# Two token parts of 256 and 264, and one 512-column matmul for the weights' high part, in a split-precision decoder step

## The chip, the cores and the metric

The kernel runs on one core of one Trainium2 chip. Its metric is the device time of one launch in microseconds (us), the median of several runs. The core has five engines that run side by side and meet at semaphores: TensorE (PE, with its weight loads shown apart as PEld), VectorE (DVE), ScalarE (ACT), GpSimd (POOL) and SyncE (SP, which issues DMAs). TensorE writes its results to PSUM, eight banks of 512 fp32 columns for each of 128 partitions; DVE and ACT read them out ("evict" them) to SBUF.

## The reference: what is computed

Two layers of a decoder trunk for 512 prompt tokens and 8 sample tokens, all in fp32. Cut to what matters here:

```python
# layer 0: x (520 x 1024)
z = x @ w_in_e            # 3592 columns: gated short convolution, mLSTM q k v, gates
out = concat(conv_part, mlstm_part) @ w_out_e
# layer 1
z = x @ w_in_o            # 2236 columns: two sparse attentions and an indexer
out = concat(o_nsa, o_dsa) @ w_out_o
# both layers
x = layer_norm(ALPHA * x + out)
x = layer_norm(ALPHA * x + square(relu(x @ w_up)) @ w_down)   # w_up 1024 x 4096
```

The products with the six weight arrays make up nearly all of the time.

## The kernel before

**Split products.** Activations and weights are each split into a high part in fp32r and a low part (the remainder, again in fp32r). A product is made of three: high weights by high activations, high weights by low activations, low weights by high activations. `split_pass` (L1010 to L1029) does this: for each of eight blocks `k` of 128 input rows and each of the three, it issues one matmul for each token half. The activations lie transposed, features on partitions and the 520 tokens along the columns, so each matmul streams 260 columns (`H2 = T // 2`). A tile, numbered `g`, is 128 output features; it takes 8 x 3 x 2 = 48 matmuls and two PSUM banks (`bank(g, half)`), one for each half, in which the three products are summed. There are 191 tiles: 29 of the even input projection (from `G_IN0`), 8 of its output projection (`G_OUT0`), 64 of the first MLP (`G_MLP0`: four chunks of 8 "up" and 8 "down" tiles), 18 of the odd input projection (`G_IN1`), 8 of its output projection (`G_OUT1`) and 64 of the second MLP (`G_MLP1`).

**Weights.** SP loads weights into the three slots of `ring`. For each tile ACT writes the high part (`w_hi`, a copy of 128x1024, at L1599), and then DVE, for some tiles POOL, writes the low part (`w_lo`, L1972), which waits for ACT's copy. `w_hi_ahead` and `w_lo_ahead` do this some tiles ahead; they stand inside the step of the tile whose results are just being evicted, so they are in line behind that eviction on their engine. `weights_here` makes PE wait for both parts.

**Evictions.** In an up tile (`hidden`) ACT takes the first half out with a relu (L1636) and DVE the second (L1996); then POOL squares in fp32 (L842), ACT squares to the high part `hh` (L1643), and DVE subtracts to get the low part `hl` (L2001). In a down or output tile (`residual`) DVE adds both halves to `xT` (L1983, L1984). In the even projection ACT copies the first half and DVE the second (L2291).

**Heads and tails.** Around a layer norm the halves run apart, so that the norm of one half lies under products of the other. `tail` runs the last tiles of a stage for the first half, then for the second. `head` runs the first tiles of the next stage for the first half; the last pieces of the second half's norm (reciprocal L2042, multiplication L2051, affine step L2068, low part L2070 on DVE; centring L808 on POOL; affine steps L1670 on ACT) stand between the evictions of the head's tiles. At an MLP's head the step of tile j for j = 0 to 3 also prepares the weights of tile j + 4.

The order on each engine is that of the code; each engine works through it in line. The matmul that all of this goes through:

```python
last = pe.matmul(bank(g, half)[0:width(g), 0:H2], w[:, k, :], x[:, k, cols(half)],
                 start=first, stop=final)
```

Of the kernel before, what the change touches and what calls it, by code (L numbers as in the profile page):

```python
# [20 lines left out]
F32 = mybir.dt.float32  # L21
# [12 lines left out]
H2 = T // 2  # L34
# [43 lines left out]
def build(nc, x_prompt, x_sample, state_conv, state_C, state_n, state_m, cache_kv, cache_idx, cache_win, page_table,  # L78
# [20 lines left out]
    with ExitStack() as ctx:  # L99
# [11 lines left out]
        with ExitStack() as mixer:  # L111
            big = mixer.enter_context(nc.sbuf_tensor("big", [P, KF, T], F32))
            ymix = mixer.enter_context(nc.sbuf_tensor("ymix", [P, KD, T], F32))
            cbuf = mixer.enter_context(nc.sbuf_tensor("cbuf", [P, 4096], F32))
        with ExitStack() as odd:

            odd.enter_context(nc.sbuf_tensor("projections", [P, len(O_NAMES) * T], F32))
            xl1 = odd.enter_context(nc.sbuf_tensor("xl1", [P, KD, T], F32R))
            odd.enter_context(nc.sbuf_tensor("behind", [P, (KF - KD - len(O_NAMES)) * T], F32))
            xh1 = odd.enter_context(nc.sbuf_tensor("xh1", [P, KD, T], F32R))  # L120


        xh = sb("xh", [P, KD, T], F32R)
        xl = sb("xl", [P, KD, T], F32R)
        hh = sb("hh", [P, KD, T], F32R)
        hl = sb("hl", [P, KD, T], F32R)
# [12 lines left out]
        def piece(n):  # L139
# [13 lines left out]
            pn_ok dsd_ev pb_mm pb_ev pt_mm pt_ev kc_ok pc_mm vf_mm vf_ev pc_n pct_mm q_sc q_mm kv_out  # L153
# [248 lines left out]

        def cols(half):
            return slice(half * H2, (half + 1) * H2)

# [14 lines left out]
        def hid_event(c, j, half=None):  # L420

            return j + KD * half if c == 0 else KD * (c + 1) + j

# [87 lines left out]
        XL = {0: xl, 1: xl1, 2: xl}  # L511
        racc = att[:, 0:T]
# [220 lines left out]
        def _(pool):  # L733
# [98 lines left out]
            def hidden(layer, g, c, j, half=None):  # L832
# [3 lines left out]
                if half != 1:  # L836
                    pool.wait_ge(sm["free_a"], g + 1)
# [22 lines left out]
            for k in range(KD):  # L860
                if k not in XE_DVE:
                    pool.wait_ge(sm["tin_a"], k + 2)
                    pool.wait_ge(sm["tin_b"], 1)
                    pool.tensor_tensor(hl[:, k, :], xT[:, k, :], xh1[:, k, :].bitcast(F32), ALU.subtract).then_inc(sm["xe_p"], 1)
# [114 lines left out]
        def _(pe):  # L979
# [32 lines left out]
            def split_pass(gs, halves, hi, lo, ready_hi=None, ready_lo=None, between=None, ks=range(KD)):  # L1012

                for g in gs:
                    weights_here(g)
                for k in ks:
                    for part, ready, x in ((0, ready_hi, hi), (0, ready_lo, lo), (1, None, hi)):
                        if ready:
                            ready(k)
                        first, final = k == ks[0] and x is hi and part == 0, k == ks[-1] and part == 1  # L1020
# [1718 lines left out]
```

## Time and profile before

| | |
|---|---|
| median of 3 runs | 1429.27 us (1426.93 to 1429.67) |
| span of the profiled execution | 1421.2 us |
| PE busy | 1366.7 us, 96% |
| DVE busy | 745.3 us, 52% |
| ACT busy | 504.6 us, 36% |
| POOL busy | 397.1 us, 28% |
| mean granted TensorE clock | 0.994 |

The span runs from the first to the last instruction of one execution; the time of a run also holds what lies around it. PE's busy time counts overlapping matmuls, so its pace is read from the distance of their starts. A row of the timeline gives the start, the duration (of several merged instructions together), the engine, the line, the operation with output and inputs, and in brackets how long the engine was idle before and who ended it.

### The profile page before, as it was taken

What the parts mean: (1) busy time and instruction counts of PE and PEld (TensorE: products, weight loads), DVE (VectorE), ACT (ScalarE), POOL (GpSimd) and SP (SyncE); (2) the same over time, 40 slices, a digit from 0 to 9 for tenths busy, and PEclk for the clock granted to TensorE, in tenths of its full rate; (3) what the DMA queues carried; (4) which work ended last, traced back from release to release, by engine and by line L of the source; (5) the groups of instructions that cost most, each with busy time, mean ns of one, the idle gap of its engine ahead of it and who ended that gap; (6) DMA issues with size and microseconds to landing.
All of it is one profiled execution on the core that took longest, in us unless ns stands there. A gap on an engine that the chain in (4) does not pass through costs nothing. (4 is left out here: it accounts for less than half of the span.)

```text
span 1421.2 us, 27641 instructions
## 1 busy us (share of the span) xinstructions
PE 1366.7 (96%) x11359; PEld 1287.3 (91%) x11359; DVE 745.3 (52%) x1378; ACT 504.6 (36%) x1004; POOL 397.1 (28%) x470
## 2 busy tenths in 40 slices
PE   6999998999999999999899999999999999999996
PEld 5999975899999999999899966667999999999996
DVE  3424777667434343343879856454774343343435
ACT  3321224345314023032542366786553032140311
POOL 3014423365101010014744473023652010010102
PEclk9999999999999999999999999999999999999998
DMA  5343170030323131312323226204113313132301
GB/s 156 125 114 107 43 238 6 3 119 31 126 83 117 63 119 60 119 60 52 60 90 60 64 82 216 61 2 120 64 56 120 119 60 119 60 119 69 110 31 60
DMA packets 87196, 123.86 MB, mean 87 GB/s; under 512 B 24438, under 2 KB 42302, under 8 KB 87040
## 3 DMA queue, kind: packets, MB, share of 16 engines
q1 hardware_dynamic: 82048, 107.00, 23.6%
q0 software_dynamic: 5024, 15.10, 3.6%
q8 instruction: 91, 1.49, 0.4%
q14 instruction: 33, 0.27, 0.1%
HBM read 115.62 MB, written 8.57 MB: 87 GB/s over the span
## 5 line engine op out<-in xcount | busy, mean ns | idle before, releaser
L1024 PE MATMUL ps<-xh,ring_lo 128*128 128x260 f32 (+2 forms) x2496 | 503.5, 283 | 1.4 <-ACT big L1599 1.4
L1024 PEld LDWEIGHTS ps<-xh,ring_lo 128*128 128x128 f32 (+2 forms) x2496 | 382.6, 187 | 3.3 <-ACT big L1599 2.3
L1024 PE MATMUL ps<-xl,wr 128*128 128x260 f32 x1568 | 351.4, 283 | 6.1 <-DVE xl L2070 3.9
L1024 PE MATMUL ps<-xh,wr 128*128 128x260 f32 x1568 | 352.9, 284 | 2.5 <-POOL xl L824 1.2
L1024 PEld LDWEIGHTS ps<-xl,wr 128*128 128x128 f32 x1568 | 255.2, 188 | 8.2 <-DVE xl L2070 5.1
L1024 PEld LDWEIGHTS ps<-xh,wr 128*128 128x128 f32 x1568 | 256.0, 188 | 5.0 <-ACT att L1636 1.4
L842 POOL TENSOR_TENSOR att<-att 128x520 f32<-128x520 f32 (+1 forms) x80 | 77.3, 967 | 548.6 <-DVE att L1996 521.5
L1972 DVE TENSOR_TENSOR ring_lo<-ring,wr 128x1024 fp32r<-128x1024 f32 (+1 forms) x144 | 192.1, 1337 | 62.1 <-ACT wr L1599 62.0
L1024 PE MATMUL ps<-hh,wr 128*128 128x260 f32 x1024 | 222.1, 283 | 0.0
L1024 PE MATMUL ps<-hh,ring_lo 128*128 128x260 f32 x1024 | 221.8, 283 | 0.0
L1024 PE MATMUL ps<-hl,wr 128*128 128x260 f32 x1024 | 221.7, 283 | 0.0
L1599 ACT ACTIVATE wr<-ring 128x1024 fp32r<-128x1024 f32 (+1 forms) x162 | 167.4, 1049 | 130.1 <-PE ps L1024 120.4
L1024 PEld LDWEIGHTS ps<-hh,wr 128*128 128x128 f32 x1024 | 164.5, 188 | 0.2 <-issue 0.2
L1024 PEld LDWEIGHTS ps<-hh,ring_lo 128*128 128x128 f32 x1024 | 164.5, 188 | 0.0
L1024 PEld LDWEIGHTS ps<-hl,wr 128*128 128x128 f32 x1024 | 164.0, 188 | 0.0
L1636 ACT ACTIVATE att<-ps 128x260 f32<-128x260 f32 x64 | 24.6, 384 | 304.4 <-PE ps L1024 304.4
L1983 DVE TENSOR_TENSOR xT<-xT,ps 128x260 f32<-128x260 f32 x96 | 37.5, 422 | 162.9 <-PE ps L1024 162.9
L1996 DVE TENSOR_SCALAR att<-ps 128x260 f32<-128x260 f32 x64 | 27.4, 428 | 137.4 <-PE ps L1024 137.4
L1024 PE MATMUL ps<-hl,ring_lo 128*128 128x260 f32 (+1 forms) x464 | 93.4, 283 | 0.0
L1599 ACT ACTIVATE big<-ps 128x260 f32<-128x260 f32 (+6 forms) x104 | 40.3, 402 | 148.5 <-PE ps L1024 133.2
L789 POOL TENSOR_TENSOR ring_lo<-ring,wr 128x1024 fp32r<-128x1024 f32 x18 | 43.3, 2412 | 109.8 <-ACT wr L1599 109.8
L986 PE MATMUL ps<-big 128*64 128x128 f32 (+3 forms) x504 | 66.7, 348 | 4.8 <-DVE small L2694 3.3
(354 smaller groups left out, 1620.8 us busy)
## 6 DMA issues: line engine op xcount, KB each, us to landing
ring<-in_w_up SPq DMA_DIRECT2D x16, 2048.0 KB, 7.9
ring<-in_w_down SPq DMA_DIRECT2D x16, 2048.0 KB, 7.9
ring<-in_w_in_e SPq DMA_DIRECT2D x9, 1024.0 KB, 5.6
ring<-in_w_in_e SPq DMA_DIRECT2D x2, 2048.0 KB, 8.8
ring<-in_w_out_e SPq DMA_DIRECT2D x2, 2048.0 KB, 8.8
ring<-in_w_in_o SPq DMA_DIRECT2D x16, 256.0 KB, 5.0
ring<-in_cache_kv POOLq DMA_DIRECT2D x32, 128.0 KB, 2.4
ring<-in_w_out_o SPq DMA_DIRECT2D x8, 512.0 KB, 8.9
```

What stands on the lines that cost most here:

```text
L789: pool.tensor_tensor(w_l, w_raw(u), w_h.bitcast(F32), ALU.subtract).then_inc(sm["w_lo_p"], 1)
L842: pool.tensor_tensor(hid[j % 2][:, cc], rel[j % 2][:, cc], rel[j % 2][:, cc], ALU.mult).then_inc(sm["hid_sq"], 1)
L986: return pe.matmul(out, lhsT, rhs, start=start, stop=stop, skip_group_check=True)
L1024: last = pe.matmul(bank(g, half)[0:width(g), 0:H2], w[:, k, :], x[:, k, cols(half)], start=first, stop=final)
L1599: return act.activation(out, in_, ACT.Copy, scale=scale)
L1636: act.activation(rel[j % 2][:, 0:H2], psA(g)[:, 0:H2], ACT.Relu).then_inc(sm["free_a"], 1)
L1972: dve.tensor_tensor(w_l, w_raw(u), w_h.bitcast(F32), ALU.subtract).then_inc(sm["w_lo"], 1)
L1983: last = (dve.tensor_tensor(x, x, y, ALU.add) if scale is None else dve.scalar_tensor_tensor(x, x, scale, y, ALU.mult, ALU.add))
L1996: dve.tensor_scalar(rel[j % 2][:, H2:T], psB(g)[:, 0:H2], 0.0, None, ALU.max).then_inc(sm["free_b"], 1)
```

## The change

The token parts become 256 and 264 columns (`HALVES`, `HW`). The high and the low activation part of a stage move into one buffer (`x2`, `h2`, `xe2`, `x12`), so that one access pattern can take both. Where `apart(g, half)` is true, for the first half of 165 of the 191 tiles, the two matmuls of the weights' high part become one of 512 columns, which writes two column ranges of one whole bank: high by high activations in one, high by low in the other. The third product adds to one of the ranges. It isn't done for the first tile of the even projection and of each MLP, the gate tile, four tiles that are scaled, and the odd input projection. The two ranges are summed at the eviction by DVE: with a reduction over pairs (`summed`), or in `residual` with a second addition. So the halves change hands: DVE takes the first half out, ACT the second, and in an up tile ACT now applies the relu to the first half in SBUF, after DVE's sum (new semaphore `rel_ok`).

```diff
-H2 = T // 2
+HALVES = (slice(0, 256), slice(256, T))
+HW = (256, T - 256)
...
+        def apart(g, half):
+
+            if half or g in (G_IN0, G_IN0 + GATE, G_MLP0, G_MLP1) or G_IN1 <= g < G_OUT1:
+                return False
+            return g >= G_OUT0 or not 16 <= E_TILE[g - G_IN0] < 20
...
                         for g in gs:
-                            w = w_split(split_of[g])[part]
+                            w = w_split(split_of[g])[part][:, k, :]
                             for half in halves:
-                                last = pe.matmul(bank(g, half)[0:width(g), 0:H2], w[:, k, :], x[:, k, cols(half)],
-                                                 start=first, stop=final)
+                                m = HW[half]
+                                out = bank(g, half)[0:width(g), 0:m]
+                                if not apart(g, half):
+                                    last = pe.matmul(out, w, x[:, n, k, cols(half)], start=first, stop=final)
+                                elif part:
+                                    last = pe.matmul(bank(g, half)[0:width(g), m:2 * m], w, x[:, hi, k, cols(half)],
+                                                     start=False, stop=final)
+                                elif n == lo:
+                                    both = bank(g, half)[0:width(g), :].rearrange("p (n t) -> p n t", n=2)
+                                    last = pe.matmul(both if hi == 0 else both[:, ::-1], w, x[:, :, k, cols(half)],
+                                                     start=k == ks[0], stop=False)
...
 # ACT, hidden
-                if half != 1:
-                    tile_done(g, 0)
+                if half != 0:
+                    tile_done(g)
+                    act.wait_ge(sm["free_b"], g)
...
-                    act.activation(rel[j % 2][:, 0:H2], psA(g)[:, 0:H2], ACT.Relu).then_inc(sm["free_a"], 1)
+                    act.activation(rel[j % 2][:, cols(1)], psB(g)[:, 0:HW[1]], ACT.Relu).then_inc(sm["free_b"], 1)
+                if half != 1:
+                    act.wait_ge(sm["free_a"], g + 1)
+                    act.activation(rel[j % 2][:, cols(0)], rel[j % 2][:, cols(0)], ACT.Relu).then_inc(sm["rel_ok"], 1)
                 if g + 1 != TAIL_OF[1]:
                     w_hi_ahead(g, 1 if half is None else half)
...
 # DVE
                 last = (dve.tensor_tensor(x, x, y, ALU.add) if scale is None
                         else dve.scalar_tensor_tensor(x, x, scale, y, ALU.mult, ALU.add))
+                if apart(g0 + m, half):
+                    link(last)
+                    last = dve.tensor_tensor(x, x, bank(g0 + m, half)[:, HW[half]:2 * HW[half]], ALU.add)
...
+            def summed(out, g, n=P):
+
+                if apart(g, 0):
+                    return dve.tensor_reduce(out, psA(g)[0:n, :].rearrange("p (n t) -> p t n", n=2), AX.X, ALU.add)
+                return dve.tensor_copy(out, psA(g)[0:n, 0:HW[0]])
...
 # DVE, hidden
-                    dve.tensor_scalar(rel[j % 2][:, H2:T], psB(g)[:, 0:H2], 0.0, None, ALU.max).then_inc(sm["free_b"], 1)
+                    summed(rel[j % 2][:, cols(0)], g).then_inc(sm["free_a"], 1)
                 if g + 1 != TAIL_OF[1]:
                     w_lo_ahead(g, 1 if half is None else half)
```

What stands in line on DVE at the head of an MLP, from the second half's variance to the second tile's step, before (L1972 is `w_lo`, L2001 `hl`, L2042 the reciprocal, L2051 the norm's multiplication):

```order
L2037 TENSOR_TENSOR att<-ps,att 128x260
L2038 TENSOR_SCALAR att<-att 128x260
L1972 TENSOR_TENSOR ring_lo<-ring,wr 128x8x128
L2001 TENSOR_TENSOR hl<-att,hh 128x260
L2042 RECIPROCAL att<-att 128x260
L2051 TENSOR_TENSOR xT<-xT,att 128x260 x2
L1972 TENSOR_TENSOR ring_lo<-ring,wr 128x8x128
L2001 TENSOR_TENSOR hl<-att,hh 128x260
```

The same place after the change (L2002 is `w_lo`, L2040 `hl`, L2081 the reciprocal, L2090 the multiplication, L2023 the new sum):

```order
L2040 TENSOR_TENSOR h<-att,h 128x256
L2081 RECIPROCAL att<-att 128x264
L2090 TENSOR_TENSOR xT<-xT,att 128x264 x2
L2023 TENSOR_REDUCE att<-ps 128x256
L2002 TENSOR_TENSOR ring_lo<-ring,wr 128x8x128
L2040 TENSOR_TENSOR h<-att,h 128x256
L2090 TENSOR_TENSOR xT<-xT,att 128x264 x2
```

The step of each head tile now begins with an eviction on DVE, ahead of `w_lo`.

ACT at the same place before (L1636 relu from PSUM, L1599 with `wr` the high weights `w_hi`, L1643 `hh`):

```order
L1636 ACTIVATE att<-ps 128x260
L1599 ACTIVATE wr<-ring 128x1024
L1643 ACTIVATE hh<-att 128x260
L1681 ACTIVATE att<-att 128x260
L1636 ACTIVATE att<-ps 128x260
L1599 ACTIVATE wr<-ring 128x1024
L1643 ACTIVATE hh<-att 128x260
```

and after (L1666 is the relu in SBUF, L1625 `w_hi`):

```order
L1707 ACTIVATE att<-ps 128x264
L1666 ACTIVATE att<-att 128x256
L1625 ACTIVATE wr<-ring 128x1024
L1673 ACTIVATE h<-att 128x256
L1711 ACTIVATE att<-att 128x264
```

The relu reads what DVE has summed, and the weights' high part stands in line behind it.

PE before, the last block of the first up chunk's last tile (second half alone) and one block `k` of a down tile with both halves:

```order
L1024 MATMUL ps<-xl,wr 128x260
L1024 MATMUL ps<-xh,ring_lo 128x260
L1024 MATMUL ps<-hh,wr 128x260 x2
L1024 MATMUL ps<-hl,wr 128x260 x2
L1024 MATMUL ps<-hh,ring_lo 128x260 x2
```

and after, one block of the down tile:

```order
L1044 MATMUL ps<-h,wr 128x264
L1050 MATMUL ps<-h,wr 128x512
L1044 MATMUL ps<-h,wr 128x264
L1046 MATMUL ps<-h,ring_lo 128x256
L1044 MATMUL ps<-h,ring_lo 128x264
```

Six matmuls of 1560 columns in all become five of 1560 columns.

## Rows read from the trace of the kernel before

**Rows 1.** The page: busy time of PE, and its granted clock in 40 slices.
```profile
PE 1366.7 (96%) x11359; PEld 1287.3 (91%) x11359; DVE 745.3 (52%) x1378; ACT 504.6 (36%) x1004; POOL 397.1 (28%) x470
...
PEclk9999999999999999999999999999999999999998
```
**Rows 2.** Busy times by stretch: PE, PEld, DVE, ACT, POOL, clock, DMA share, GB/s.
```profile
400.00:500.00 100.00, 100.00 (x834) 100.00 (x833) 37.27 (x51) 21.86 (x31) 8.43 (x8) 1.00 0.24 85
```
**Rows 3.** Timeline of DVE in the up tiles of an MLP chunk.
```profile
414.77 0.43 DVE L1996 TENSOR_SCALAR att<-ps 128x260 f32<-128x260 f32 x1 [3.99 <-PE ps L1024]
416.02 1.45 DVE L1972 TENSOR_TENSOR ring_lo<-ring,wr 128x1024 fp32r<-128x1024 f32 x1 [0.82 <-ACT wr L1599]
...
455.14 0.43 DVE L1996 TENSOR_SCALAR att<-ps 128x260 f32<-128x260 f32 x1 [2.46 <-PE ps L1024]
...
457.76 0.69 DVE L2001 TENSOR_TENSOR hl<-att,hh 128x520 fp32r<-128x520 f32 x1
```
**Rows 4.** Timeline of PE in the mLSTM: plain fp32 matmuls of several widths.
```profile
235.66 1.02 PE L986 MATMUL ps<-att 128*128 128x512 f32 x2
236.52 0.59 PE L986 MATMUL ps<-big 128*128 128x256 f32 x2
236.96 0.81 PE L986 MATMUL ps<-att,ones 128*128 128x384 f32 x2
237.60 0.81 PE L986 MATMUL ps<-att 128*128 128x384 f32 x2
```
**Rows 5.** Timeline of PE: from the gate tile (8 weight columns) to full tiles.
```profile
30.24 0.63 PE L1024 MATMUL ps<-xh,ring_lo 128*8 128x260 f32 x4
...
31.42 0.40 PE L1024 MATMUL ps<-hl,ring_lo 128*128 128x260 f32 x2
...
35.04 0.40 PE L1024 MATMUL ps<-hl,ring_lo 128*128 128x260 f32 x2
```
**Rows 6.** Groups of DVE instructions: a reduction of 512 elements.
```profile
L2429 DVE TENSOR_REDUCE small<-att 128x8 f32<-128x512 f32 x2 | 1.4, 686 | 0.1
```
**Rows 7.** Timeline of DVE at the head of the second MLP.
```profile
1037.75 0.43 DVE L2037 TENSOR_TENSOR att<-ps,att 128x260 f32<-128x260 f32 x1 [5.32 <-ACT att L1677]
...
1038.98 1.61 DVE L1972 TENSOR_TENSOR ring_lo<-ring,wr 128x1024 fp32r<-128x1024 f32 x1
...
1044.48 1.77 DVE L1972 TENSOR_TENSOR ring_lo<-ring,wr 128x1024 fp32r<-128x1024 f32 x1
...
1049.51 1.22 DVE L1972 TENSOR_TENSOR ring_lo<-ring,wr 128x1024 fp32r<-128x1024 f32 x1
...
1053.43 1.22 DVE L1972 TENSOR_TENSOR ring_lo<-ring,wr 128x1024 fp32r<-128x1024 f32 x1
```
**Rows 8.** Timeline of ACT at the same place.
```profile
1037.61 0.39 ACT L1636 ACTIVATE att<-ps 128x260 f32<-128x260 f32 x1
1037.87 1.07 ACT L1599 ACTIVATE wr<-ring 128x1024 fp32r<-128x1024 f32 x1
1038.82 0.43 ACT L1643 ACTIVATE hh<-att 128x260 fp32r<-128x260 f32 x1
```
**Rows 9.** PE's waits: waiter, who ended it, total us, times, longest.
```profile
PE ps L1024 <- DVE ring_lo L1972: 1.0, 2, 0.5
```
**Rows 10.** Timeline of DVE in the even projection's last tiles.
```profile
175.55 0.42 DVE L2291 COPY big<-ps 128x260 f32<-128x260 f32 x1
...
205.09 0.19 DVE L2312 TENSOR_TENSOR small<-small 128x32 f32<-128x32 f32 x1
```
**Rows 11.** Timeline of DVE in the first half of the even output tail.
```profile
279.38 1.25 DVE L1972 TENSOR_TENSOR ring_lo<-ring,wr 128x1024 fp32r<-128x1024 f32 x1 [1.44 <-ACT wr L1599]
280.56 0.75 DVE L1984 SCALAR_TENSOR_TENSOR xT<-xT,ps 128x260 f32<-128x260 f32 x2
```
**Rows 12.** Busy times by stretch, columns as in rows 2.
```profile
826.00:828.00 2.00, 0.53 (x4) 0.29 (x2) 1.82 (x7) 0.70 (x3) 0.59 (x2) 1.00 0.07 8
828.00:835.00 7.00, 6.58 (x35) 4.90 (x35) 1.96 (x8) 3.20 (x10) 7.00 (x11) 0.52 0.01 1
```

More of the change, by code:

```diff
@@ L114, in build @@
             cbuf = mixer.enter_context(nc.sbuf_tensor("cbuf", [P, 4096], F32))
+        with ExitStack() as even:
+            even.enter_context(nc.sbuf_tensor("projected", [P, (KF - KD) * T], F32))
+            xe2 = even.enter_context(nc.sbuf_tensor("xe2", [P, 2, KD, T], F32R))
         with ExitStack() as odd:
             odd.enter_context(nc.sbuf_tensor("projections", [P, len(O_NAMES) * T], F32))
[L118 to L126, printed above, removed]
+            x12 = odd.enter_context(nc.sbuf_tensor("x12", [P, 2, KF - len(O_NAMES), T], F32R))
+        x2 = sb("x2", [P, 2, KD, T], F32R)
+        h2 = sb("h2", [P, 2, KD, T], F32R)
+        xel, xeh = xe2[:, 0], xe2[:, 1]
+        xl1, xh1 = x12[:, 0], x12[:, 1]
+        xh, xl = x2[:, 0], x2[:, 1]
+        hh, hl = h2[:, 0], h2[:, 1]
         sb("gap", [P, KD * T + 4096 - NWS * KD * P])
@@ L1010, in weights_here, with split_pass @@
                 pe.wait_ge(sm[by], n)
-            def split_pass(gs, halves, hi, lo, ready_hi=None, ready_lo=None, between=None, ks=range(KD)):
+            def split_pass(gs, halves, x, order=(0, 1), ready_hi=None, ready_lo=None, between=None, ks=range(KD)):
+                hi, lo = order
                 for g in gs:
@@ L1029, in split_pass, with split_tile @@
                         between()
-            def split_tile(g, hi, lo, ready=None, between=None):
+            def split_tile(g, x, order=(0, 1), ready=None, between=None):
                 banks_free(g)
-                split_pass((g,), (0, 1), hi, lo, ready, between=between)
+                split_pass((g,), (0, 1), x, order, ready, between=between)
             def x_hi_here(n_ln, half):
@@ L1067, in head @@
                 first = n // 2
-                split_pass(range(g, g + first), (1,), XH[n_ln], XL[n_ln], x_hi_here(n_ln, 1), x_lo_here(n_ln, 1))
+                split_pass(range(g, g + first), (1,), *X[n_ln], x_hi_here(n_ln, 1), x_lo_here(n_ln, 1))
                 for i in range(first, n):
@@ L1203, in _ @@
                     for half in range(2):
-                        last = mm(ps[4 + half][0:4, 0:H2], ident[0:8, 4:8], gz[:, half * H2:(half + 1) * H2])
+                        last = mm(ps[4 + half][0:4, 0:HW[half]], ident[0:8, 4:8], gz[:, cols(half)])
                     last.then_inc(sm["fg_mm"], 1)
@@ L1313, in _ @@
                 if idx >= 4:
-                    split_tile(G_IN1 + idx, xh1, xl1, between=selected if idx == 4 else None)
+                    split_tile(G_IN1 + idx, x12, (1, 0), between=selected if idx == 4 else None)
                 if idx == 4:
@@ L1675, in moments @@
                 act.wait_ge(sm["stats_mm"], 2 * n_ln + half + 1)
-                copy(mu[:, cols(half)], ps[4 * half][:, 0:H2]).then_inc(sm["mu_ok"], 1)
-                act.activation(var[:, cols(half)], ps[4 * half][:, 0:H2], ACT.Square).then_inc(sm["sq_mu"], 1)
+                copy(mu[:, cols(half)], ps[4 * half][:, 0:HW[half]]).then_inc(sm["mu_ok"], 1)
+                act.activation(var[:, cols(half)], ps[4 * half][:, 0:HW[half]], ACT.Square).then_inc(sm["sq_mu"], 1)
             def deviation(n_ln, half):
@@ L1726, in _ @@
             act.wait_ge(sm["tin_b"], 1)
-            copy(xh1[:, :, S:T], xT[:, :, S:T]).then_inc(sm["tin_a"], 1)
+            copy(xeh[:, :, S:T], xT[:, :, S:T]).then_inc(sm["tin_a"], 1)
             for k in range(KD):
@@ L1750, in _ @@
                     act.wait_ge(sm["small_in"], 16 * 2)
[L1751 removed]
+                    act.activation(gz[:, cols(1)], psB(g)[0:8, 0:HW[1]], ACT.Identity, bias=gbc[0:8, :]).then_inc(sm["free_b"], 1)
                 else:
[L1753 removed]
+                    copy(big[:, home, cols(1)], psB(g)[:, 0:HW[1]], MH_SCALE if 16 <= t < 20 else 1.0).then_inc(sm["free_b"], 1)
                 w_hi_ahead(g)
@@ L1990, in hidden @@
                 cc = slice(0, T) if half is None else cols(half)
-                if half != 0:
-                    tile_done(g)
+                if half != 1:
+                    tile_done(g, 0)
                     if e >= 2:
```

81 lines of the change are left out of this document (41 added, 40 removed).

## The prediction

> **What bounds the kernel now.** First the page: PE is busy for 96% of the span at full granted clock [rows 1], so the question is what sets PE's pace and where it stands still. In a stretch of the first MLP PE issues 834 matmuls in 100 us with no gap, while DVE is busy for 37 us and ACT for 22 [rows 2]: there only PE counts. A finer pace comes from DVE's evictions of up tiles, which follow PE. From the first to the last of eight there are 40.37 us, seven tiles of 48 matmuls, so 5.767 us a tile and **120.15 ns a matmul** of 260 columns, 720.9 ns for the six of a block k [rows 3]. Second, where PE isn't alone: the heads of the two MLPs, where DVE works almost without a pause from 1037.75 on, with weight preparation, low parts and the second half's norm in one line [rows 7], and PE already waits for `w_lo` there, once in each head, 0.5 us each [rows 9]; and the last tiles of the even projection, where DVE runs as closely from 175.55 to 205.09 [rows 10]. At these places the change adds work to DVE.
>
> **What PE gains.** 165 tiles have 8 blocks each, so 1320 matmuls go, but no column goes: 1560 a block before and after. All hangs on how the 120.15 ns divide into a part for each instruction and a part for each column; the trace has one width of fp32r alone. Plain fp32 matmuls give a scale: start to start 0.43 us for 512 columns, 0.32 for 384, 0.22 for 256 [rows 4], so time by the column, 0.84 ns each, and next to nothing fixed. If fp32r streams at half of that, 260 columns are 109 ns (108.3 at one column in each cycle of the 2.4 GHz level), and 11.8 ns a matmul are left. If those are fixed, a block goes from 720.9 to 650 + 5 x 11.8 = 709 ns and **saves 11.9 ns**. If they belong to the columns it saves 0. Weight loads have a small share: with 8 weight columns ten matmuls take 1.18 us, 118 ns each, and thirty at 128 weight columns 3.62 us, 120.7 ns [rows 5]; with one load fewer this alone gives 2.7 ns. In the other direction the one long matmul may hide its neighbours' cost too: if the 512 columns ran with the 2 ns of the plain kind, the block would save 240.3 x 512/520 - 215.5 = 21 ns, and if its neighbour gained as well about 30. I take 11.9, between the ends 0 and 30, since the plain rows are the nearest and half their slope is what one column a cycle needs. The Trainium skill ("TensorE: Matmul & The Clock Gate", section "Back-to-back issue gap") gives N/2.4 plus about 2.5 ns for a stream of matmuls. The plain rows agree with so small a fixed part [rows 4]; fp32r at 120 ns doesn't follow it. By that rule the block would save 2.5 ns only. It speaks against the change and is the second case below.
>
> The gain counts where PE sets the pace. In the MLPs these are 126 tiles less the 14 merged ones in the heads: 112 x 8 = 896 blocks, **-10.7 us**. Both halves' evictions fit there: a tile takes 5.7 us, and DVE's work of 2.6 us in an up tile grows by 0.3.
>
> **The eviction in a steady up tile.** DVE's sum reads 512 elements; the nearest row is a reduction of 512 at 0.69 us [rows 6] against 0.43 for the copy it replaces. Then ACT's relu and, behind it, `w_hi`, then DVE's `w_lo` and `hl`. From the last eviction to the end of `hl` there are 3.31 us now [rows 3]. New: 0.69 + 0.03 + 0.28 (relu, start to next start) + 1.05 + 0.06 + 1.37 + 0.69 = 4.2 us. The down tile that follows reads this last part at its eighth block, after 7 x 0.709 = 5.0 us. Covered, with 0.8 us left; a sum of over 1.5 us would show eight times.
>
> **The heads: what DVE and ACT lose.** Before, ACT ran ahead with relu and `w_hi` (1037.61 and 1037.87 [rows 8]), and DVE came to a `w_lo` that could start at once. Now each head step on DVE is: sum, then wait until ACT has done the relu and `w_hi`, then `w_lo`. Nothing hides this bubble, since DVE works in line and ACT waits for DVE's sum. Bubble: 0.03 + 0.27 (1037.61 to 1037.87) + 1.05 + 0.06 = 1.41 us. The first tile isn't merged: copy 0.42 + 1.41 = 1.83 us. Tiles 1 to 3: 0.69 + 1.41 = 2.10 us each. The `w_lo` of step 3, which PE needs for tile 7, ended at 1053.43 + 1.22 = 1054.65 [rows 7]; PE was waiting for it. It comes 1.83 + 3 x 2.10 = 8.1 us later. PE is held at tile 5 (the `w_lo` of step 1 comes 3.9 us late), at tile 6 and at tile 7, its own gain of 0.1 us a tile is lost in the waits but for tile 7, and the second half starts 8.0 us late. From there PE isn't held again: the last low parts of the norm come about as much later as the second half starts later, and PE reads them at the end of a pass over four tiles of 4 x 24 x 122 ns = 11.7 us. Behind DVE's waits are also queued the norm's multiplications, but PE reads them later. Both MLP heads have the same row of steps: 2 x 8.0 = **+16.0 us**. Bounds: if the sum took 0.43 us (the present eviction) 2 x 7.2, if it took 1.2 (as long as the reductions' 512 elements twice over, less one overhead) 2 x 9.5.
>
> **The even projection.** 23 merged tiles. PE gains 17 x 8 x 11.9 ns = 1.6 us up to tile 22; then DVE's line sets the time. Six evictions from 175.55 to 205.09 [rows 10] grow by 0.27 us each, 1.6 us, and the two before take some of PE's lead. I count **+0.9 us**; bounds -1.5 (DVE's growth hidden) and +4 (a sum of 1.2 us).
>
> **The output tails.** In their first half a DVE step is now residual, wait for ACT's square and `w_hi`, `w_lo`: 3.0 us a step, of which the wait is 1.44 [rows 11]. The second addition adds 0.45 us, so the `w_lo` of step 3 ends 1.8 us later, at 282.4; PE reaches that tile at 282.45. PE keeps 6 x 8 x 11.9 = 0.57 us in each of two tails: **-1.1 us**. The last tile's residual is later by 0.45 and earlier by 0.6, and the norm's chain under the second half stays as it is. The second half isn't merged; its 264 columns against 260 are in the block's sum.
>
> **The sum.** -10.7 + 16.0 + 0.9 - 1.1 = +5.1 us on the span of 1421.2, so 1426.3. The median lies 8.1 above the span, 1429.27; on it the forecast is **1434.4 us**. (A measurement can tell about 0.2%, 2.9 us.)
>
> **The rivals.**
> - *The cost goes by columns.* Saving 0 to 5 ns a block: PE gains 0 to 4.5 us in the MLPs where I took 10.7, and 0 to 0.5 in place of 1.1 in the tails: 1441 at 5 ns, 1446 at 0. For it: the plain rows scale by columns. Against: half their slope doesn't reach 120 ns.
> - *The long matmul pays more than its own instruction (faster).* The mechanism is in PE's stream: while 512 columns run, the next weights are there early and the neighbours' 11.8 ns shrink. The heads cost 16.0 all the same. The sum is zero at 896s = 15.8 us, s = 17.6 ns a block; it is faster by over 0.2% from s = 21. At 21 it is 1426, at 30 some 12 us less than now less the tails, 1417. For it: the load starts with the matmul before it and lasts about as long as 260 columns; against: with 8 weight columns the pace is only 2.7 ns better.
> - *The heads' line isn't as I read it.* If DVE reached its sums while ACT's copies were already made, only the sums would count: 2 x (0.42 + 3 x 0.69) = 5.0 in place of 16, 1423. Against: the order after the change puts `w_hi` behind the relu, and the relu behind the sum.
> - *The clock falls in the heads.* After a stretch in which PE was busy 0.53 of 2.0 us the granted clock went to 0.52 for 7 us [rows 12], to the 1.2 GHz level. In the heads PE now stands for three times 3 to 4 us. A fall while it runs tile 7 and the group pass costs half of the time, 3.4 us a head: 1438 to 1441.
>
> **How the numbers follow.** The forecast as it stands, 1432.2 to 1438 with the bounds of the reduction's length: 0.35. Costs by column 0.14, the clock 0.09; with the forecast, all above 1432.2, that makes **slower 0.58**. Savings of 14 to 21 ns a block, or heads somewhat better than I read them, end within 0.2%: **same 0.22**. The long matmul's case beyond 21 ns 0.12 and the heads' case 0.08: **faster 0.20**. The range: above I leave out the purest column case (under 0.1), below the last of the faster cases (under 0.1): **1422 to 1445**.
>
> **What would show it.** PE: the distance of up-tile evictions in the steady MLP, 5.767 us now, should be 5.67; 5.73 or more means columns, 5.60 or less the faster case. The 512-column matmul, start to start: 225 ns, or 230 and more. DVE: a TENSOR_REDUCE of about 0.69 us, and in each MLP head four gaps of 1.4 us ended by ACT's `wr`. PE: three waits for DVE's `ring_lo` in each head, some 10 us together, where one of 0.5 us stood. The even projection's DVE line ends within a microsecond of 205. The clock row at 1.0 in the heads. I am wrong if the head gaps are hidden, if the reduction takes over 1 us, or if the pace moves by more than 0.17 us a tile or not at all.

## The result

The changed kernel takes **1439.3 us** (median of 4 runs, 1438.03 to 1442.34), the kernel before 1428.8 in the runs beside it (4 runs, 1426.93 to 1429.67): a ratio of 1.0086, 95% interval 1.0064 to 1.0108, so 10.5 us are added where the forecast had 5.1. The time is inside the range and on the side forecast. The profiled spans are 1421.2 and 1436.4 us, 15.2 apart.

The page of the changed kernel, busy times and granted clock in 40 slices, against [rows 1]:

```profile
PE 1370.4 (95%) x10039; PEld 1229.3 (86%) x10039; DVE 788.0 (55%) x1458; ACT 531.1 (37%) x1068; POOL 394.8 (27%) x470
...
PEclk9999999999999999999999999999999999999998
```

1320 matmuls have gone and PE is busy no shorter. The steady part of the first MLP, against [rows 2] (PE, PEld, DVE, ACT, POOL, clock, DMA share, GB/s) and, in the timeline of DVE, against [rows 3]:

```profile
400.00:500.00 100.00, 100.00 (x702) 93.84 (x701) 42.25 (x63) 24.06 (x38) 8.44 (x8) 1.00 0.27 97
```
```profile
424.64 0.69 DVE L2023 TENSOR_REDUCE att<-ps 128x256 f32<-128x512 f32 x1 [3.37 <-PE ps L1046]
426.76 1.23 DVE L2002 TENSOR_TENSOR ring_lo<-ring,wr 128x1024 fp32r<-128x1024 f32 x1 [1.43 <-ACT wr L1625]
427.91 0.69 DVE L2040 TENSOR_TENSOR h<-att,h 128x520 fp32r<-128x520 f32 x1
...
464.63 0.69 DVE L2023 TENSOR_REDUCE att<-ps 128x256 f32<-128x512 f32 x1 [1.75 <-PE ps L1046]
```

Seven tiles from 424.64 to 464.63 are 39.99 us: 5.713 us a tile, where it was 5.767. A block costs 714.1 ns instead of 720.9, and **6.8 ns are saved** where the forecast had 11.9. From start to start on PE, over the up and down tiles between 410 and 650 us, the 512-column matmuls take 232.2 ns on average (225 forecast), those of 264 columns 121.9 and those of 256 columns 116.8; in the kernel before 260 columns take 120.2. The sum takes the 0.69 us forecast, and `hl` ends 3.96 us after the sum starts (4.2 forecast), under PE's work.

DVE's timeline in the head of the second MLP, against [rows 7]:

```profile
1048.74 0.43 DVE L2076 TENSOR_TENSOR att<-ps,att 128x264 f32<-128x264 f32 x1 [5.37 <-ACT att L1707]
1049.21 0.30 DVE L2077 TENSOR_SCALAR att<-att 128x264 f32<-128x264 f32 x1
1049.42 0.42 DVE L2024 COPY att<-ps 128x256 f32<-128x256 f32 x1
1051.27 1.56 DVE L2002 TENSOR_TENSOR ring_lo<-ring,wr 128x1024 fp32r<-128x1024 f32 x1 [1.43 <-ACT wr L1625]
...
1055.48 0.78 DVE L2090 TENSOR_TENSOR xT<-xT,att 128x264 f32<-128x264 f32 x2
1056.17 0.68 DVE L2023 TENSOR_REDUCE att<-ps 128x256 f32<-128x512 f32 x1
1058.29 1.50 DVE L2002 TENSOR_TENSOR ring_lo<-ring,wr 128x1024 fp32r<-128x1024 f32 x1 [1.44 <-ACT wr L1625]
...
1065.31 1.23 DVE L2002 TENSOR_TENSOR ring_lo<-ring,wr 128x1024 fp32r<-128x1024 f32 x1 [1.43 <-ACT wr L1625]
...
1070.39 1.50 DVE L2002 TENSOR_TENSOR ring_lo<-ring,wr 128x1024 fp32r<-128x1024 f32 x1 [1.43 <-ACT wr L1625]
```

The four waits for ACT's `wr` are there, 1.43 or 1.44 us each. PE's waits for `w_lo` (waiter, who ended it, total us, times, longest), and PE's timeline at the three of the first head (0.72, 3.71 and 2.30 us; the second head has two, 0.72 and 3.71, and the sixth, 0.42, stands at 1011 us in the odd output tail):

```profile
PE ps L1050 <- DVE ring_lo L2002: 11.6, 6, 3.7
```
```profile
333.14 0.47 PE L1050 MATMUL ps<-x,wr 128*128 128x512 f32 x1 [0.72 <-DVE ring_lo L2002]
...
339.89 0.47 PE L1050 MATMUL ps<-x,wr 128*128 128x512 f32 x1 [3.71 <-DVE ring_lo L2002]
...
345.23 0.77 PE L1050 MATMUL ps<-x,wr 128*128 128x512 f32 x1 [2.30 <-DVE ring_lo L2002]
345.79 0.41 PE L1046 MATMUL ps<-x,ring_lo 128*128 128x256 f32 x1
346.00 0.63 PE L1050 MATMUL ps<-x,wr 128*128 128x512 f32 x1
```

After the third wait the 512-column matmuls start 0.64 us after one another together with their neighbour, where before the wait it was 0.35: the granted clock has fallen to the 1.2 GHz level. Three stretches at that level, columns as in rows 2 with the length of the stretch first (two more, 3.4 us at 204.9 and the last 9.5 us of the span, lie where PE has little to do):

```profile
344.80:348.20 3.40, 2.97 (x9) 2.62 (x10) 2.67 (x7) 1.45 (x4) 0.17 (x1) 0.51 0.02 5
1065.00:1071.80 6.80, 5.12 (x16) 4.30 (x16) 5.02 (x8) 5.07 (x10) 1.35 (x3) 0.50 0.00 0
822.70:836.40 13.70, 13.70 (x72) 11.22 (x71) 4.52 (x15) 4.83 (x16) 5.41 (x10) 0.50 0.08 14
```

**Where the 15.2 us of span are.** The marks are starts on DVE: its first subtraction of the mLSTM's scores, the first step of each half's variance (L2037 before, L2076 after), and the first and last of its custom instructions in the attention stage.

| stage | before | after | difference | of which |
|---|---|---|---|---|
| start to the scores (even projection) | 206.6 | 208.3 | +1.7 | 0.7 lies ahead of PE's wait near 50 us, 1.0 behind it |
| to the variance, half 0 (mLSTM, output tail) | 83.7 | 84.6 | +0.9 | the tail |
| to half 1 | 29.0 | 29.0 | 0 | |
| to the next norm (first MLP) | 359.4 | 364.2 | +4.8 | 448 blocks -3.05; head +7.8 |
| odd projection, two marks | 133.9 | 133.7 | -0.2 | |
| attention | 159.9 | 162.4 | +2.5 | clock low for 13.7 us, before for 6.8 [rows 12] |
| to the variance (odd output tail) | 36.2 | 37.5 | +1.3 | the tail |
| to half 1 | 29.0 | 29.0 | 0 | |
| second MLP to the end | 383.5 | 387.7 | +4.2 | 448 blocks -3.05; head and the rest +7.3 |

The changed kernel's profiled run took 1438.03 us, 1.6 above its span and 1.3 below its median. The span of before lies 7.6 us below the median beside it, so if the same 1.6 us lie around it, its profiled run was some 6 us faster than the median. That is why medians differ by less than spans. Most of the spread among runs of one kernel goes with the mean granted clock: of 23 runs of the kernel before that stood beside the last timed experiments, those at 0.987 took 1431.4 to 1432.6 us, those at 0.991 1426.9 to 1429.6, those at 0.995 1422.1 and 1423.4. Single microseconds are therefore read from stages in the traces, not from medians.

### The profile page after: what moved, and what is told of

It reads as the page before. It is cut to its first block and busy times, and to the rows that moved or that the text cites. A ratio compares the mean times of both kernels' runs of the same rounds, so it can differ in the third digit from the quotient of the medians.

```text
span 1436.4 us, 25209 instructions
## 1 busy us (share of the span) xinstructions
PE 1370.4 (95%) x10039; PEld 1229.3 (86%) x10039; DVE 788.0 (55%) x1458; ACT 531.1 (37%) x1068; POOL 394.8 (27%) x470
## 5 line engine op out<-in xcount | busy, mean ns | idle before, releaser
L1044 PE MATMUL ps<-x,wr 128*128 128x264 f32 (+3 forms) x1888 | 410.0, 285 | 5.7 <-DVE x L2109 3.7
L1044 PEld LDWEIGHTS ps<-x,wr 128*128 128x128 f32 (+1 forms) x1888 | 306.0, 187 | 9.2 <-DVE x L2109 4.9
L1044 PE MATMUL ps<-h,wr 128*128 128x264 f32 x1024 | 271.9, 284 | 0.0
L1050 PE MATMUL ps<-x,wr 128*128 128x512 f32 x624 | 239.7, 401 | 12.9 <-DVE ring_lo L2002 11.6
L1044 PE MATMUL ps<-x,ring_lo 128*128 128x264 f32 (+3 forms) x944 | 240.6, 284 | 0.0
L2002 DVE TENSOR_TENSOR ring_lo<-ring,wr 128x1024 fp32r<-128x1024 f32 (+1 forms) x144 | 181.3, 1263 | 106.3 <-ACT wr L1625 106.1
L1625 ACT ACTIVATE wr<-ring 128x1024 fp32r<-128x1024 f32 (+1 forms) x162 | 167.0, 1046 | 112.1 <-PE ps L1044 97.8
L1050 PE MATMUL ps<-h,wr 128*128 128x512 f32 x512 | 197.8, 394 | 0.6 <-DVE h L2040 0.6
L1044 PEld LDWEIGHTS ps<-h,wr 128*128 128x128 f32 x1024 | 186.3, 188 | 0.1
L1046 PE MATMUL ps<-x,ring_lo 128*128 128x256 f32 x624 | 173.2, 282 | 0.0
L1044 PEld LDWEIGHTS ps<-x,ring_lo 128*128 128x128 f32 (+1 forms) x944 | 165.7, 187 | 0.0
L1044 PE MATMUL ps<-xe,ring_lo 128*128 128x264 f32 (+2 forms) x840 | 158.0, 287 | 1.9 <-DVE big L2023 1.9
L1046 PEld LDWEIGHTS ps<-x,ring_lo 128*128 128x128 f32 x624 | 119.1, 191 | 18.4
L1050 PEld LDWEIGHTS ps<-h,wr 128*128 128x128 f32 x512 | 96.3, 188 | 5.1 <-issue 0.9
```

What stands on the lines that cost most here:

```text
L1044: last = pe.matmul(out, w, x[:, n, k, cols(half)], start=first, stop=final)
L1046: last = pe.matmul(bank(g, half)[0:width(g), m:2 * m], w, x[:, hi, k, cols(half)], start=False, stop=final)
L1050: last = pe.matmul(both if hi == 0 else both[:, ::-1], w, x[:, :, k, cols(half)], start=k == ks[0], stop=False)
L1625: return act.activation(out, in_, ACT.Copy, scale=scale)
L2002: dve.tensor_tensor(w_l, w_raw(u), w_h.bitcast(F32), ALU.subtract).then_inc(sm["w_lo"], 1)
```

## The experiments

**The parts alone.** The changed kernel with the halves of 256 and 264 and with its new order of evictions, but no matmul merged:

```diff
 def apart(g, half):
-    if half or g in (G_IN0, G_IN0 + GATE, G_MLP0, G_MLP1) or G_IN1 <= g < G_OUT1:
-        return False
-    return g >= G_OUT0 or not 16 <= E_TILE[g - G_IN0] < 20
+    return False
```

> The changed kernel without any 512-column matmul: parts of 256 and 264 tokens, six matmuls a block, the evictions in their new hands (DVE takes the first half out with a copy or one addition, ACT the second, and in an up tile ACT applies the relu to the first half in SBUF behind DVE's copy). Theory (the heads' line on DVE and ACT costs the time, the long matmul gives some back): a tile of an MLP at the old 5.77 us, no gain on PE, and in each MLP head four steps of 0.42 + 1.43 us, 7.4 us a head; in all some 1443 us, 14 over the kernel before. Rival (it is the sums of two ranges, the extra DVE reading, that cost): without them the time is that of the kernel before, 1429.

1441.8 us (6 runs), ratio 1.0097 (1.0066 to 1.0128). By the medians the merging itself gains 2.5 us over this kernel. By the stages it gains 0.7 and 3.3 us in the two MLPs, and loses 1.0 in the even projection and 1.2 and 1.6 in the two output tails, so next to nothing in the sum. What loses against the kernel before is the new order: the two MLP stages take 364.9 and 391.0 us, where they took 359.4 and 383.5. The steady pace, 5.77 us a tile, is that of before. DVE, up tiles:

```profile
420.32 0.42 DVE L2022 COPY att<-ps 128x256 f32<-128x256 f32 x1 [3.87 <-PE ps L1042]
422.17 1.23 DVE L2000 TENSOR_TENSOR ring_lo<-ring,wr 128x1024 fp32r<-128x1024 f32 x1 [1.43 <-ACT wr L1623]
...
426.08 0.42 DVE L2022 COPY att<-ps 128x256 f32<-128x256 f32 x1 [2.07 <-PE ps L1042]
```

**Merging off in the heads only**, the order as in the changed kernel:

```diff
-    if half or g in (G_IN0, G_IN0 + GATE, G_MLP0, G_MLP1) or G_IN1 <= g < G_OUT1:
+    if half or g in (G_IN0, G_IN0 + GATE) or G_IN1 <= g < G_OUT1:
+        return False
+    if G_MLP0 <= g < G_MLP0 + KD or G_MLP1 <= g < G_MLP1 + KD:
         return False
```

> The changed kernel with the 512-column matmul off in the first half of the eight head tiles of each MLP; the line of DVE, ACT and the weights there is as in the changed kernel. Theory (the bubble of DVE waiting for ACT's relu and high weights is the larger part, the longer sum the smaller): each of three head steps gets 0.27 us shorter, 0.8 us a head, some 1437.7 us. Rival (the sum itself is what the heads lose): most of the 11 us come back, 1430.

1436.5 us (12 runs), ratio 1.0050 (1.0030 to 1.0069). Nearer to the theory, though the two MLP stages are only 0.6 and 0.3 us shorter, where 0.8 each were expected. PE still waits 9.5 and 0.4 us for `ring_lo`: with plain copies most of the loss stays, since the four waits of 1.43 us a head stay.

**ACT makes `w_hi` ahead of the relu**, merging as in the changed kernel:

```diff
+                if half == 0:
+                    w_hi_ahead(g, 0)
                 if half != 1:
                     act.wait_ge(sm["free_a"], g + 1)
...
-                if g + 1 != TAIL_OF[1]:
+                if half != 0 and g + 1 != TAIL_OF[1]:
                     w_hi_ahead(g, 1 if half is None else half)
```

> The changed kernel with one move: in the first half of an MLP head ACT makes the next high weights (w_hi) before it waits for DVE's sum and applies the relu, not behind it. Everything else, the sums and the 512-column matmuls too, stays. Theory (the bubble is the price): four bubbles of 1.43 us a head go, 5.7 us a head, 11.4 in all, so some 1428 us; no gap of 1.43 us ended by ACT's wr is left on DVE in the heads. Rival (DVE's own work bounds the heads): under 3 us come back, 1437.

1426.3 us (12 runs), ratio 0.9995 (0.9970 to 1.0020). By the medians the move gives 13 us back. The two MLP stages take 358.2 and 383.0 us, where the changed kernel has 364.2 and 387.7: **10.7 us** less, 11.4 expected, of which 1.4 is the low clock of the first head. Another 2.6 us lie in the attention stage, where the clock was low for 6.8 us and not for 13.7; they aren't the move's. The kernel is level with the one before. DVE in its first head: `w_lo` follows the copy at once, and in each step only a wait of 0.5 us for POOL's square is left. PE still waits for `w_lo` twice in each head, 2.3 us together, where the kernel before has 0.5.

```profile
322.46 0.42 DVE L2026 COPY att<-ps 128x256 f32<-128x256 f32 x1
322.79 1.21 DVE L2004 TENSOR_TENSOR ring_lo<-ring,wr 128x1024 fp32r<-128x1024 f32 x1
324.51 0.97 DVE L2042 TENSOR_TENSOR h<-att,h 128x256 fp32r<-128x256 f32 x1 [0.50 <-POOL att L858]
```

**Columns or instructions.** At the end of the changed kernel PE also runs seven trains of 32 fp32r matmuls, each matmul with weights of its own and the other engines nearly idle (so the kernel does more than the reference asks):

```diff
+for s, k in probe:
+    pe.matmul(ps[6][:, 0:256], wr[:, s, k, :], flow[:, 520 * k:520 * k + 256], ...)
```

> The changed kernel with seven trains of 32 fp32r matmuls each, added at the end behind PE's last transposes, when the other engines are nearly idle: 260, 512, 512 in two ranges, 384 and 256 columns with 128 weight columns, then 260 and 512 columns with 8 weight columns, new weights each time. Fixed-cost theory: about 12 ns over N/2.4 at every width, 225 ns at 512 and 118 at 256. Column theory: 0.45 ns a column at every width, 232 at 512, 174 at 384, 116 at 256. If other engines' traffic or the weight loads made the difference, the trains run at N/2.4 + 2 ns: 215 at 512, and with 8 weight columns faster than with 128.

PE's timeline, a row for each train (32 matmuls; starts 231.9 ns apart where a train of 512 columns takes 7.42 us to the next one's start):

```profile
1424.46 4.08 PE L1617 MATMUL ps<-ring_lo,wr 128*128 128x260 f32 x32
1428.39 7.59 PE L1619 MATMUL ps<-ring_lo,wr 128*128 128x512 f32 x32
1435.81 7.59 PE L1621 MATMUL ps<-ring_lo,wr 128*128 128x512 f32 x32
1443.25 5.73 PE L1623 MATMUL ps<-ring_lo,wr 128*128 128x384 f32 x32
1448.82 3.95 PE L1625 MATMUL ps<-ring_lo,wr 128*128 128x256 f32 x32
1452.61 3.98 PE L1627 MATMUL ps<-ring_lo,wr 128*8 128x260 f32 x32
1456.42 7.57 PE L1629 MATMUL ps<-ring_lo,wr 128*8 128x512 f32 x32
```

Start to start: 512 columns 231.9 ns, read as one range or as two (L1619, L1621); 384 columns 5.57 us / 32 = 174.1; 256 columns 3.79 / 32 = 118.4; and with 8 weight columns 260 take 3.81 / 32 = 119.1, with 128 of them 119.9 (after the train's first matmul, which overlaps the transposes). That is 0.453, 0.453 and 0.463 ns a column for 512, 384 and 256: **nearly all of the cost goes by columns**. The 512 and 384 columns match the column theory (232 and 174), the 256 alone the fixed-cost theory's 118. Two of 256 are 236.8 ns, one of 512 231.9, so merging saves 4.9 ns in a train, and not the 11.8 of the forecast. Whether one range is read or two makes no difference, and 8 weight columns instead of 128 make 0.8 ns at 260 columns.

**The heads as before the change** (ACT evicts the first half, no merging in the heads), the rest as changed:

```diff
+                if half == 0:
+                    tile_done(g, 0)
+                    act.activation(rel[j % 2][:, cols(0)], psA(g)[:, 0:HW[0]], ACT.Relu).then_inc(sm["free_a"], 1)
...
-                if half != 1:
+                if half is None:
...
                     summed(rel[j % 2][:, cols(0)], g).then_inc(sm["free_a"], 1)
```

> The changed kernel, but the heads of the two MLPs work as in the kernel before: their tiles are not merged, and ACT makes the relu of the first half out of PSUM, ahead of w_hi, while DVE evicts nothing there. The rest is merged as in the changed kernel. Theory: e3_whi_first (1426.25 us) still has DVE's copy and three sums in the line of each head, 2.5 us of waits on w_lo where the kernel before has 0.5; taking them out gives 2 x 2.0 us back, and the heads' own merging gain of 2 x 7 x 8 x 6.8 ns = 0.8 us is lost: 1423. What is left against before is the gain of the steady MLP (6.1 us) less what the even projection and the output tails lose (1.7 + 2.2). Rival: what was left of the heads' loss in e3 is hidden by the norm under them, so that nothing more comes back: 1426 to 1427, as e3. The ratio to before is 0.996 by the theory and 0.9985 by the rival.

1428.0 us (12 runs), ratio 0.9996 (0.9980 to 1.0012): the median sides with the rival. The stages side with the theory: the two MLP stages take 356.7 and 381.5 us, against 358.2 and 383.0 with `w_hi` first, 3.0 us less (3.2 expected), and against 359.4 and 383.5 before. In the profiled run the difference is eaten elsewhere, by a clock that was low for 3.4 us at 212, 253, 700 and 840 us and for 13.7 at 820. By its median this kernel equals the one before; the heads' cost is shown by the stages. Against the changed kernel they are 7.5 and 6.2 us shorter.

**The output tails unmerged too**:

```diff
+    if G_OUT0 <= g < G_OUT0 + KD or G_OUT1 <= g < G_OUT1 + KD:
+        return False
```

> e5_heads_as_before, and the first half of the two output tails isn't merged either. Theory: after the second addition DVE hands the last x tiles over so late that the sums of the norm (POOL's chain) hold PE when it has done the first tile of the second half; without merging this wait of 1.1 us goes, and each tail ends 1.2 to 1.6 us earlier (0.90 + 0.27 and 1.26 + 0.35, the stage differences of the changed kernel and of e1_split_only against before): 2.8 us less than e5, about 1420. Rival, the line of the prediction: the norm's chain is not delayed and merging gains 0.4 us in each tail, so that the time rises by 0.7 us, to about 1424. Shown by the wait of norm_sums on att, 1.1 us in the first tail, and by the two stages' length.

**1422.5 us** (6 runs), ratio 0.9958 (0.9941 to 0.9974): faster than both kernels. The odd tail's stage goes from 37.5 to 35.9 us. PE's wait for the norm's sums, here and, second, in the kernel with tails merged:

```profile
PE ps L1008 <- POOL att L821: 0.4, 2, 0.2
```
```profile
PE ps L1006 <- POOL att L819: 2.1, 4, 0.9
```

The odd tail's 1.6 us are what was expected of it. In the even tail's stage both profiled runs have stretches of low clock, so that its part can't be read. 5.5 us between the medians are more than the 2.8 expected, and the mean clock doesn't explain it: the runs at 0.990 take 1426.5 to 1428.9 us there and 1421.8 to 1423.2 here. What makes up the rest stays open. Against the kernel before the gain is safer: the runs at 0.991 take 1420.9 and 1422.2 us here, and 1426.9 to 1429.6 there.

**Merging in the steady MLPs alone** (the even projection unmerged as well):

```diff
-    return g >= G_OUT0 or not 16 <= E_TILE[g - G_IN0] < 20
+    return G_MLP0 <= g < G_MLP0 + 2 * KF or g >= G_MLP1
```

> e6_tails_off, and the even projection isn't merged either: matmuls are merged only in the MLPs outside their heads. Theory: DVE's copies of 0.43 in place of sums of 0.69 in the last tiles of the even projection bring its end from 208.3 back to the 206.8 of e1_split_only, 1.5 us less than e6: about 1418.5, ratio to before 0.992, faster than both kernels. The step at the first score, 206.6 in the kernel before, tells it. Rival: PE's gain of 17 tiles x 8 x 6.8 ns = 0.9 us in the first tiles is lost with it and the stage's end is set by something else, so that the time stays at e6's within 0.5 us.

1423.0 us (12 runs, 1416.7 to 1427.8), ratio 0.9965 (0.9944 to 0.9986): again faster than both, but no different from the one before, where 1.5 us less were expected. From the start of PE's wait near 50 us to the scores it takes 156.8 us, against 157.8 in the kernels that merge there and 156.8 before: the even projection's merging costs 1.0 us, and this run began that stretch 1.7 us later than the other (50.9 against 49.3). That start lies anywhere from 49.3 to 51.4 us in the profiled kernels, with merging there and without.

**What DVE's instructions cost beside POOL.** In the heads the `w_lo` of step 3 came 6.2 us late, not 8.1, though each step grew as forecast. Two kernels, each with POOL's centring in the heads cut to 8 columns (this part of the computation is left out), the first from the kernel before, the second from the changed one:

```diff
-                        centre(n_ln, 1, range(4 * j, 4 * j + 4))
+                        for m in range(4 * j, 4 * j + 4):
+                            pool.wait_ge(sm["mu_ok"], 2 * n_ln + 2)
+                            pool.tensor_tensor(xT[:, m, T - 8:T], xT[:, m, T - 8:T], mu[:, T - 8:T],
+                                               ALU.subtract).then_inc(sm["cen_p"], 1)
```

> The kernel before, but in the heads of the two MLPs POOL subtracts the mean in the last 8 columns of the second half instead of all 260 (eight instructions a head; this part of the computation is left out). Theory: while POOL's four subtractions of 4.1 to 4.4 us run, DVE's instructions beside them take up to twice their time (w_lo 1.61 and 1.77 us against 1.22 without, hl 0.97 against 0.42, the pair on xT 1.36 and 1.73 against 0.77). Without them the w_lo of step 3 ends about 3.6 us earlier after the second half's variance than now: 13.3 us instead of 16.9, and PE's wait for ring_lo in the heads goes (0.3 us left at most). Rival: those DVE instructions take their time by themselves (the first touch of new tiles), whatever POOL does: 16.9 us stays. The time itself moves by 1 us or less either way.

> The changed kernel with the same cut: POOL subtracts the mean in the last 8 columns of the second half only, in the heads of the MLPs. In the changed kernel the w_lo of step 3 ends 23.15 us after the variance, 6.2 later than in the kernel before, where the four steps grow by 1.85 + 3 x 2.11 = 8.2. Theory: the missing 2 us are DVE's time beside POOL that the waits of 1.43 us have taken over; with the cut DVE's instructions are short in both kernels, so this one saves only some 2.9 us (23.15 to 20.2) against 3.6 of the kernel before, and the difference between the two comes nearer to 8.2 (7 or more). Rival: POOL has no part in it, the end stays at 23.15 and the difference at 6.2. The sum of the four waits for ACT's wr stays at 4 x 1.43 by both.

DVE's timeline in the second head, from the variance to the `w_lo` of step 3; the kernel before with the cut, then the changed one with it:

```profile
1039.33 0.43 DVE L2040 TENSOR_TENSOR att<-ps,att 128x260 f32<-128x260 f32 x1 [5.33 <-ACT att L1680]
...
1040.56 1.23 DVE L1975 TENSOR_TENSOR ring_lo<-ring,wr 128x1024 fp32r<-128x1024 f32 x1
1041.71 0.42 DVE L2004 TENSOR_TENSOR hl<-att,hh 128x260 fp32r<-128x260 f32 x1
...
1043.85 0.77 DVE L2054 TENSOR_TENSOR xT<-xT,att 128x260 f32<-128x260 f32 x2
...
1051.47 1.21 DVE L1975 TENSOR_TENSOR ring_lo<-ring,wr 128x1024 fp32r<-128x1024 f32 x1
```
```profile
1046.51 0.43 DVE L2079 TENSOR_TENSOR att<-ps,att 128x264 f32<-128x264 f32 x1 [5.38 <-ACT att L1710]
...
1065.39 1.50 DVE L2005 TENSOR_TENSOR ring_lo<-ring,wr 128x1024 fp32r<-128x1024 f32 x1 [1.43 <-ACT wr L1628]
```

From the variance to the end of that `w_lo` there are 13.35 us (13.3 expected; 16.9 uncut) and 20.38 (20.2 expected; 23.15 uncut). The difference rises from 6.25 to 7.0. A `w_lo` of 1.61 us becomes 1.23 and `hl` 0.42 instead of 0.97: **these DVE instructions take longer beside POOL's**. The rival falls. Of the 1.2 us that are still missing to 8.2, most lie where POOL's squares and low parts run beside DVE in the first kernel and not in the second (two affine steps of 0.71 and 0.72 us against 0.40 and 0.42, a low part of 0.85 against 0.43). No wait of PE for `ring_lo` is left in the heads of the first kernel, as expected; its two MLP stages are 0.8 us shorter each than before. The Trainium skill ("SBUF — State Buffer", section "Who interferes with whom") has the same rule: a DVE instruction with two SBUF inputs contends with a GpSimd instruction that reads SBUF, and one blocks the other. These rows agree for `w_lo`, `hl` and the multiplications on `xT`. The times were 1423.6 and 1434.6 us, with 1428.1 for the kernel before beside them, in a single run each, which tells nothing of single microseconds.

The first of these kernels, which has nothing of the change, also ran 13.7 us at the low clock in the attention stage:

```profile
814.50:828.20 13.70, 13.70 (x72) 11.22 (x71) 4.46 (x15) 4.64 (x16) 5.27 (x10) 0.50 0.07 14
```

Its attention stage takes 162.4 us as well, and with `w_hi` first, where the clock was low for 6.8 us, it takes 159.8. So that row of the table above, 2.5 us, isn't the change's. The heads differ: in the five profiled kernels whose heads hold PE for 1.9 to 3.7 us at a time (the changed one, the first two experiments, the one with the trains, the last), the clock falls once in each head; in the six without such holds, in none.

## Why the prediction was right, and where it was not

**What PE gains (mis-sized).** 896 blocks by 6.8 ns are 6.1 us, not 10.7. The failed step is the split of 120.15 ns into 108.3 by column and 11.8 fixed. The slope of plain fp32 [rows 4] was halved, and that doesn't hold: fp32r has a slope of its own, about 0.45 ns, and little that is fixed. The rival of the columns had 0 to 5 ns a block; trains give 4.9, the kernel 6.8, nearer to it than to the forecast. Why the kernel saves 1.9 ns more than the trains is not shown. For the faster rival the forecast had a weight load last about as long as 260 columns; its rows last 0.19 us, against 0.12 from one matmul to the next. By the rule of the Trainium skill ("TensorE: Matmul & The Clock Gate", section "Back-to-back issue gap"), N/2.4 plus about 2.5 ns, 512 columns would take 215.8 ns and the block save 2.5. The prediction took it for a stream; that section gives it for a matmul by itself, and about 131 ns at 512 columns for a stream of weight loads and matmuls. The measured 231.9 and 118.4 ns follow neither; the small fixed part is nearer to the truth than mine.

**The steady eviction (right).** Sum 0.69, wait 1.43, `hl` done in 3.96 us. One thing was missed: in the last chunk of the second MLP the first two down tiles start as a pair of the tail, and PE reaches the low part earlier. It waits 0.6 us for `hl` there.

**The heads (right in mechanism, somewhat less).** The bubble was 1.43 us (1.41 forecast), the steps grow by 1.85 and 3 x 2.11 (1.83 and 2.10). The end of the fourth `w_lo` came 6.25 us late and not 8.1: behind the waits POOL's centring runs by itself, and DVE's later instructions are shorter (0.78 us for a pair on `xT` where it was 1.36, 1.50 for the second `w_lo` where it was 1.77 [rows 7]). The forecast moved the old durations unchanged. PE's waits are 6.7 us in the first head and 4.4 in the second, not 10. In the sum: 7.8 and about 6.7, together 14.5 where 16.0 stood, of which 1.4 is the clock. The kernel with its heads as before gives nearly the same by another way: its stages are 7.5 and 6.2 us shorter than the changed kernel's. The 1.36 is this row of the kernel before:

```profile
1043.20 1.36 DVE L2051 TENSOR_TENSOR xT<-xT,att 128x260 f32<-128x260 f32 x2
```

**The clock (a rival that came on top).** It fell in both heads, as that rival had it, but at less cost than its 3.4 us a head. In the first the low stretch starts 0.4 us before the third wait ends. The five pairs of matmuls behind the wait take 3.20 us, where the same five behind the second wait take 1.82: it costs 1.4. In the second it lies over tile 6, and PE's slow tile only fills what would have been the third wait: none is left there, since the `w_lo` sets the end either way. The kernel with the trains, the same as the changed one up to its end, bears this out: its first head has a low stretch of 6.8 us over tile 6, no third wait, and a first MLP stage of 362.8 us, 1.4 less than the 364.2 above.

**The even projection (right).** +1.0 us behind PE's wait near 50, +0.9 forecast. PE's last wait there, for DVE's copy before and for its sum after (total us, times, longest), and DVE's line after:

```profile
PE ps L986 <- DVE big L2291: 0.7, 1, 0.7
```
```profile
PE ps L1002 <- DVE big L2023: 2.1, 1, 2.1
```

```profile
201.54 0.69 DVE L2023 TENSOR_REDUCE big<-ps 128x256 f32<-128x512 f32 x1
...
206.84 0.19 DVE L2351 TENSOR_TENSOR small<-small 128x32 f32<-128x32 f32 x1
```

DVE's line ends at 206.84 against 205.09 [rows 10], not within a microsecond, for 0.7 of it was there already when PE's wait near 50 us began.

**The output tails (wrong, sign and all).** Forecast -1.1, measured +0.9 and +1.3. The step that failed is "the norm's chain under the second half stays as it is". PE's gain didn't reach the end, because the last tiles' residuals were no longer in PE's time but in DVE's. Before, POOL's last addition ended at 287.85, 0.65 us before PE came for it:

```profile
287.10 0.75 POOL L801 TENSOR_TENSOR att<-att 128x260 f32<-128x260 f32 x1
```

DVE, then POOL, then PE, in the changed kernel:

```profile
284.04 0.41 DVE L2014 SCALAR_TENSOR_TENSOR xT<-xT,ps 128x256 f32<-128x256 f32 x1
284.49 0.42 DVE L2017 TENSOR_TENSOR xT<-xT,ps 128x256 f32<-128x256 f32 x1
```
```profile
285.05 0.74 POOL L814 TENSOR_TENSOR att<-att,xT 128x256 f32<-128x256 f32 x1 [2.02 <-DVE xT L2017]
...
290.28 0.73 POOL L817 TENSOR_TENSOR att<-att 128x256 f32<-128x256 f32 x1
```
```profile
291.06 1.13 PE L1002 MATMUL ps<-att,meanM 128*128 128x256 f32 x4 [0.84 <-POOL att L817]
```

The step of tile 3 holds DVE until 284.04, so tiles 4 to 6 follow at its own pace. POOL needs 1.52 us for each of its pairs of additions and has four left from 285.05, to 291.0. PE has done the first tile of the second half by 290.2 and waits 0.84 us; in the odd tail it waits 0.87, and 0.42 more at 1011 us for a `w_lo`, which the forecast had ready in time. Without merging in the tails these three waits are gone. I had looked at the last tile's residual (rightly on time) and not at the queue that feeds POOL.

**The whole.** Forecast -10.7 + 16.0 + 0.9 - 1.1 = +5.1. Measured -6.1 + 14.5 + 1.0 + 2.2 + 0.6 = +12.2 in the spans; 2.5 of the attention's clock and 0.7 at the start come to it, less 0.2 in the odd projection. By the medians it is +10.5. The 0.6 is the wait for `hl`. The sign came from the heads, and they were read right; that the error stayed at 5 us is partly luck, since the heads' loss and PE's gain had both been put too high.

## What to carry to other kernels

Merging matmuls is worth what a train of each width says, and here it says 2% of a pair; measure the width before counting instructions. When an engine that both evicts and prepares weights takes over the first step of a chain, look for what now stands behind it: moving ACT's `w_hi` in front of its relu was worth 10.7 us in the two MLP stages, more than the 6.1 us that merging saves PE in them. And merge only where nobody waits for the eviction: outside heads and output tails, with the heads as before, it gives 0.4% over the kernel before.

## What the runs showed of the hardware

In trains at the 2.4 GHz level an fp32r matmul costs 0.453 ns a column from 384 columns on (231.9 ns at 512, with one range or two), and 512 columns take about the same with 8 weight columns as with 128. Two multiplications of 128x260 with both inputs in SBUF take DVE 0.77 us with POOL at rest and up to 1.74 beside it. A granted clock that fell to the 1.2 GHz level for 3.4 us cost 1.4 us where PE had work, and one of 6.8 us nothing where PE would have waited for DVE anyway: the mean clock of a run doesn't say what it cost. What makes it stay low for 13.7 us instead of 6.8 in the attention stage, in both kernels, I leave open.
